# Expert loop of a two-layer encoder: the down product set behind the next block's up product and computed from high and low parts

## What is computed

```python
def expert_block(args):
    xb, e = args
    h = jax.nn.silu(xb @ w_gate[e]) * (xb @ w_up[e])
    return h @ w_down[e]
```

## Time and profile before

| | |
|---|---|
| median of three runs (lowest, highest) | 2327.24 us (2322.62 to 2336.02) |
| the profiled execution's own time | 2328.09 us |
| its span, from first to last instruction | 2326.4 us |
| PE busy, share of the span | 94% |
| DVE, ACT, POOL busy | 57%, 43%, 8% |
| mean granted TensorE clock | 0.967 |
| HBM traffic over the span | 171 GB/s |

### The profile page before, as it was taken

One profiled execution on the slowest core, in us unless ns is written; L12 is line 12 of the kernel. 1 busy time (PEld: TensorE's weight loads), 2 busy tenths in 40 slices (PEclk: granted clock), 3 DMA queues, 4 the chain that ended last, 5 costly groups with the idle time before them and its releaser, 6 DMA issues.

```text
span 2326.4 us, 35484 instructions
## 1 busy us (share of the span) xinstructions
PE 2177.5 (94%) x13296; PEld 1830.2 (79%) x13296; DVE 1320.5 (57%) x2102; ACT 992.8 (43%) x1649; POOL 196.2 (8%) x236
## 2 busy tenths in 40 slices
PE   8899988999999899999788999899999989999998
PEld 7778957989889677777687886598988877777774
DVE  2775476533244766666767746835314466666667
ACT  2355565123332255555235547612323224555553
POOL 0000011000000331000200001100000022200004
PEclk9899989999999899999899999899999989999999
DMA  4045111232100599999511112123211038999996
GB/s 156 37 157 192 37 73 56 73 109 73 56 26 35 193 377 374 380 378 363 209 55 37 37 37 92 38 73 104 78 37 55 37 148 322 376 379 375 379 379 237
DMA packets 78548, 385.64 MB, mean 166 GB/s; under 512 B 10472, under 2 KB 11864, under 8 KB 43608
## 3 DMA queue, kind: packets, MB, share of 16 engines
q1 hardware_dynamic: 55264, 327.83, 37.6%
q0 software_dynamic: 10096, 30.38, 3.6%
q10 hardware_dynamic: 13064, 25.75, 3.0%
HBM read 352.79 MB, written 46.07 MB: 171 GB/s over the span
## 4 chain that ended last, share of the span: by engine, by line
PE 77%; DVE 12%; ACT 7%; issue 2%; DMA 1%; DVEq 0%; POOL 0%; ACTq 0%; SPq 0%; POOLq 0%
PE bank L2116 37%; PE bank L2593 10%; PE bank L2567 9%; PE bank L2557 8%; PE bank L2448 2%; DVE weight_slots_parts L1380 2%; PE bank L2132 2%; PE bank L2402 1%; PE bank L2533 1%; ACT x_transposed L1062 1%; PE bank L2285 1%; ACT weight_slots_parts L914 1%; PE bank L2256 1%; ACT scratch L1018 1%; DVE scratch L1532 1%
## 5 line engine op out<-in xcount | busy, mean ns | idle before, releaser
L2116 PE MATMUL bank<-weight_slots_parts,x_transposed_parts 128*128 128x256 f32 x2496 | 466.6, 289 | 4.5 <-ACT mixer_region L965 2.8
L2116 PEld LDWEIGHTS bank<-weight_slots_parts,x_transposed_parts 128*128 128x128 f32 x2496 | 397.0, 196 | 5.5 <-ACT mixer_region L965 3.2
L1824 DVE TENSOR_TENSOR weight_slots_parts<-weight_slots,mixer_region_parts 128x2048 fp32r<-128x2048 f32 x140 | 321.3, 2314 | 85.9 <-ACT mixer_region_parts L1207 85.8
L1207 ACT ACTIVATE mixer_region_parts<-weight_slots 128x2048 fp32r<-128x2048 f32 x140 | 261.0, 1909 | 23.7 <-ACT x_transposed L1282 18.1
L2116 PE MATMUL bank<-x_transposed_parts,weight_slots_parts 128*128 128x512 f32 (+1 forms) x1024 | 266.5, 348 | 1.8 <-DVE mixer_region L1489 1.8
L1380 DVE TENSOR_TENSOR weight_slots_parts<-weight_slots,weight_slots_parts 128x2048 fp32r<-128x2048 f32 x58 | 132.9, 2292 | 223.5 <-ACT weight_slots_parts L914 223.0
L2593 PE MATMUL bank<-weight_slots,x_transposed 128*128 128x512 f32 x560 | 246.4, 593 | 0.0
L2567 PE MATMUL bank<-mixer_region_parts,x_transposed_parts 128*128 128x256 f32 x1120 | 207.3, 283 | 0.4 <-DVE weight_slots_parts L1824 0.4
L2116 PEld LDWEIGHTS bank<-x_transposed_parts,weight_slots_parts 128*128 128x128 f32 x1024 | 183.4, 196 | 24.4 <-DVE mixer_region L1489 3.3
L2557 PE MATMUL bank<-mixer_region_parts,x_transposed_parts 128*128 128x512 f32 x560 | 193.0, 416 | 5.6 <-DVE x_transposed_parts L1829 5.6
L2593 PEld LDWEIGHTS bank<-weight_slots,x_transposed 128*128 128x128 f32 x560 | 103.4, 190 | 117.9 <-issue 101.7
(11 more groups left out here) (311 smaller groups left out, 3565.7 us busy)
## 6 DMA issues: line engine op xcount, KB each, us to landing
weight_slots<-in_w_gate SPq DMA_DIRECT2D x70, 1024.0 KB, 7.3
weight_slots<-in_w_up SPq DMA_DIRECT2D x70, 1024.0 KB, 7.1
weight_slots<-in_w_down SPq DMA_DIRECT2D x70, 1024.0 KB, 7.6
weight_slots<-in_w_in SPq DMA_DIRECT2D x20, 1024.0 KB, 5.0
slots_y<-x_transposed ACTq DMA_DIRECT2D x66, 256.0 KB, 7.2
weight_slots<-in_wkv_mem SPq DMA_DIRECT2D x16, 1024.0 KB, 4.9
slots_y<-in_consts SPq DMA_DIRECT2D x6, 2304.0 KB, 18.1
weight_slots<-in_w_out SPq DMA_DIRECT2D x8, 1024.0 KB, 5.1
```

What stands on the lines that cost most here:

```text
L1207: nc.scalar.activation(hi, raw, ACT.Copy).then_inc(moe.high_ready, 1)
L1824: v.tensor_tensor(lo, raw, hi.bitcast(F32), ALU.subtract).then_inc(moe.low_ready, 1)
L2116: ins = pe.matmul(ps, lhs[i](k), rhs[j](k), start=k == 0 and a == 0, stop=k == ks - 1 and a == 2)
```

## The change

PE's order in a block becomes gate(b), up(b), the transposes of the next block's rows, down of block b-1, the transposes of `hb` of block b. The first block has no down, and the last one runs gate, down(b-1), up, the transposes, down(b). Down is made of three products of high and low parts like the others, so the two down parts and the turned hidden rows are split as well: ACT makes six high parts in a block and DVE six low ones. Up goes over two halves of the contraction with 512 columns each, in one bank, so the gated product is one instruction. ACT copies both halves of the output. Every raw part of down is loaded when down of block b-1 has let go of its place, one block ahead of its use, except in the last block, whose down parts go into gate's places. `SLOT_ORDER` changes which place the first units of layer 1 use; the loads of layer 1's "q0" and the gather of the stored outputs wait for the shifted counts (`y_stored` by 32 more).

```diff
 
 X_STATS = (50, 58, 84)
+
+DOWN_HI = 3584, G_HI + 2 * KD * KVG
 
...
+SLOT_ORDER = ((0, 1, 2), (1, 0, 2))
 LAST_OF = {key: n for n, (name, key) in enumerate(UNITS)}
 
 
...
         def slot_of(name):
-            return (now[0] * len(UNITS) + UNIT[name]) % SLOTS
+            return SLOT_ORDER[now[0]][UNIT[name] % SLOTS]
...
         hb = xt_t[:, 2560:3072]
-        hbT = xt_t[:, 3072:3584].rearrange("p (k t) -> p k t", k=4)
+        hbT_hi = xt_parts[:, 3072:3584].rearrange("p (k t) -> p k t", k=4)
+        hbT_lo = xt_parts[:, 5632:6144].rearrange("p (k t) -> p k t", k=4)
         yb = xt_t[:, 3584:4608]
...
             o = 4096 * slot_of(("wx0", "wx1", "wx2")[i // 2]) + 2048 * (i % 2)
-            k = (4, 4, KD, KD, 4, 4)[i]
-            return by_k(ring[:, o:o + 2048], k), by_k(ring_parts[:, o:o + 2048], k), by_k(mix_parts[:, 2048 * i:2048 * i + 2048], k)
+            if i < 4:
+                hi = mix_parts[:, 2048 * i:2048 * i + 2048]
+            else:
+                hi = (y_parts, mix_parts)[i - 4][:, DOWN_HI[i - 4]:DOWN_HI[i - 4] + 2048]
+            return by_k(ring[:, o:o + 2048], 4), by_k(ring_parts[:, o:o + 2048], 4), by_k(hi, 4)
...
                     def load_up(e, h, signal):
-                        sp.dma_start(expert_part(2 + h)[0], by_k(w_up[l, e, h])).then_inc(signal, 16)
-
-                    def load_down(e, h, signal):
-                        sp.dma_start(expert_part(4 + h)[0], by_k(w_down[l, e, h], 4)).then_inc(signal, 16)
+                        sp.dma_start(expert_part(2 + h)[0], by_k(w_up[l, e][:, 2048 * h:2048 * h + 2048], 4)).then_inc(signal, 16)
+
+                    def load_down(e, h, signal, part=4):
+                        sp.dma_start(expert_part(part + h)[0], by_k(w_down[l, e, h], 4)).then_inc(signal, 16)
...
                     sp.wait_ge(ids_ready, 1 * l + 1)
                     n_blocks = sp.value_load(r_nbi[0:1, 0:1], min_val=NE, max_val=BLOCKS)
-                    with sp.Fori(1, n_blocks) as b:
+                    sp.sem_inc(moe.dl_loaded, 16)
...
+                    with sp.Fori(1, n_blocks - 1) as b:
+                        e = sp.value_load(r_bei[0:1, bass.ds(b + 1, 1)], min_val=0, max_val=NE - 1)
+                        sp.wait_ge(moe.ga_done, b + 1)
+                        load_gate(e, 0, moe.ga_loaded)
+                        sp.wait_ge(moe.g_filled, b + 2)
+                        load_gate(e, 1, moe.gb_loaded)
+                        sp.wait_ge(moe.ua_done, b + 1)
+                        load_up(e, 0, moe.ul_loaded)
+                        sp.wait_ge(moe.u_filled, b + 2)
+                        load_up(e, 1, moe.ur_loaded)
                         e = sp.value_load(r_bei[0:1, bass.ds(b, 1)], min_val=0, max_val=NE - 1)
-                        sp.wait_ge(moe.ga_done, b)
...
+                        sp.wait_ge(moe.y_filled, 2 * b + 2)
                         load_down(e, 0, moe.dl_loaded)
-                        sp.wait_ge(moe.y_filled, 2 * b + 1)
+                        sp.wait_ge(moe.y_filled, 2 * b + 3)
                         load_down(e, 1, moe.dr_loaded)
+                    e = sp.value_load(r_bei[0:1, bass.ds(n_blocks - 1, 1)], min_val=0, max_val=NE - 1)
+                    sp.wait_ge(moe.ga_done, n_blocks)
+                    load_down(e, 0, moe.ga_loaded, 0)
+                    sp.wait_ge(moe.g_filled, n_blocks + 1)
+                    load_down(e, 1, moe.gb_loaded, 0)
...
+                    def silu(b):
                         act.wait_ge(moe.h_done, b + 1)
                         act.wait_ge(moe.g_filled, b + 2)
                         nc.scalar.activation(gact, banks[2][:, :], ACT.Silu).then_inc(moe.g_ready, 1)
+                    def high_hidden(blocks):
+                        act.wait_ge(moe.hT_filled, blocks + 1)
+                        nc.scalar.activation(hbT_hi[:, :, :], banks[4][:, :].rearrange("p (k t) -> p k t", k=4),
+                                             ACT.Copy).then_inc(moe.hT_high_ready, 1)
+
+                    def store_output(blocks, y_at, h):
+                        if h == 0:
+                            act.wait_ge(moe.y_stored, 32 * blocks + 32)
+                        w = slice(512 * h, 512 * h + 512)
+                        ready = (moe.yl_ready, moe.yr_ready)[h]
+                        act.wait_ge(moe.y_filled, 2 * blocks + 2 + h)
+                        nc.scalar.activation(y_at[:, w], banks[5 + h][:, :], ACT.Copy).then_inc(ready, 1)
+                        act.wait_ge(ready, blocks + 2)
+                        act.dma_start(by_block[blocks - 1, :, w], y_at[:, w]).then_inc(moe.y_stored, 16)
+
+                    def high_down(blocks, part=4):
+                        split_part(part, moe.dl_loaded, blocks + 1)
+                        split_part(part + 1, moe.dr_loaded, blocks + 1)
+
+                    def expert_block(b, first):
+                        if not first:
+                            high_hidden(b)
+                            high_down(b)
+                        silu(b)
+                        split_part(0, moe.ga_loaded, b + 2)
+                        split_part(1, moe.gb_loaded, b + 2)
+                        act.wait_ge(moe.xT_filled, 2 * b + 4)
+                        block_xT()
+                        split_part(2, moe.ul_loaded, b + 2)
+                        if not first:
+                            store_output(b, yb, 0)
+                        split_part(3, moe.ur_loaded, b + 2)
+                        if not first:
+                            store_output(b, yb, 1)
+
+                    expert_block(0, True)
+                    with act.Fori(1, n_blocks - 1) as b:
                         expert_block(b, False)
-                    expert_block(n_blocks - 1, True)
+                    b = n_blocks - 1
+                    high_hidden(b)
+                    high_down(b)
+                    silu(b)
+                    split_part(0, moe.ga_loaded, n_blocks + 1)
+                    store_output(b, yb, 0)
+                    store_output(b, yb, 1)
+                    split_part(1, moe.gb_loaded, n_blocks + 1)
+                    act.wait_ge(spread_turned, l + 1)
+                    act.wait_ge(moe.u_filled, n_blocks + 1)
+                    nc.scalar.activation(spread_t[:, :], banks[0][:, 0:NSPREAD * P], ACT.Copy).then_inc(spread_ready, 1)
+                    high_hidden(n_blocks)
+                    if l < DEPTH - 1:
+                        now[0] = l + 1
+                        split("q0")
+                        now[0] = l
+                    for h in range(2):
+                        store_output(n_blocks, last_yb, h)
+                    if l < DEPTH - 1:
+                        now[0] = l + 1
+                        split("q1")
+                        now[0] = l
...
-                    def expert_block(b, last):
+                    def low_hidden(blocks):
+                        dve.wait_ge(moe.hT_high_ready, blocks + 1)
+                        v.tensor_tensor(hbT_lo[:, :, :], banks[4][:, :].rearrange("p (k t) -> p k t", k=4),
+                                        hbT_hi[:, :, :].bitcast(F32), ALU.subtract).then_inc(moe.hT_ready, 1)
+
+                    def gated(b):
                         dve.wait_ge(moe.g_ready, b + 2)
-                        dve.wait_ge(moe.ul_filled, b + 1)
-                        v.tensor_tensor(hb[:, 0:256], gact[:, 0:256], banks[3][:, 0:256], ALU.mult).then_inc(moe.hl_done, 1)
                         dve.wait_ge(moe.u_filled, b + 2)
-                        v.tensor_tensor(hb[:, 256:512], gact[:, 256:512], banks[7][:, 0:256], ALU.mult).then_inc(moe.h_done, 1)
-                        if not last:
-                            low_block_xT(b + 1)
-                            low_part(0, 4 * b + 5)
...
+                    def expert_block(b, first):
+                        if not first:
+                            low_hidden(b)
+                            low_part(4, 6 * b + 11)
+                            low_part(5, 6 * b + 12)
+                        low_part(0, 6 * b + 13)
+                        gated(b)
+                        low_part(1, 6 * b + 14)
+                        low_block_xT(b + 1)
+                        low_part(2, 6 * b + 15)
+                        low_part(3, 6 * b + 16)
+
...
+                    expert_block(0, True)
+                    with dve.Fori(1, n_blocks - 1) as b:
                         expert_block(b, False)
-                    expert_block(n_blocks - 1, True)
+                    b = n_blocks - 1
+                    low_hidden(b)
+                    low_part(4, 6 * b + 11)
+                    low_part(5, 6 * b + 12)
+                    low_part(0, 6 * b + 13)
+                    low_part(1, 6 * b + 14)
+                    gated(b)
+                    low_hidden(n_blocks)
...
+                    add_stored(0)
+                    add_stored(1)
+                    if l < DEPTH - 1:
+                        low_weights("q0")
```

(103 more changed lines are left out.)

126 lines of the change are left out of this document (37 added, 89 removed).

## The result

The changed kernel takes 2353.61 us (median of 6 runs, 2346.24 to 2357.47) beside 2330.77 for the one before: ratio 1.0093, 95% interval 1.0073 to 1.0113, so 22 us slower. The forecast was 2314, 13 us under the 2327.24 it was made against. The profiled execution took 2348.95 us with a span of 2347.1, against 2328.1 and 2326.4 before: 20.7 us of span to explain.

The account below looks back on a forecast made before the run. PE was taken to bound the expert loop, with DMA near; a period of 18.4 instead of 19.42 us over 31 blocks gave -31.6, first blocks -2, tails +20: 2314.5 from 2328.1, median 2314, range 2290 to 2343.

Parts of the forecast that it names:

- PE's own period, 17.78: In the expert loop, PE's work per block: three products at 5.49 us plus transposes 1.31, 1.64 less than before.
- The chain through one weight part, 11.5 + L: Expert loop, gate's second half released, loaded, split, reused: 11.5 us plus load landing L, taken as 6.8, gives 18.3.
- The DMA bound, 18.2: Expert loop transfers: 7.30 MB a block takes 16.9 us at 431 GB/s; leaving half of today's loss gives 18.2.
- rival C: Expert loop: DMA becomes the bound, period stays 19.3 to 19.4 us, tails unpaid, 2344 us in all; chance 0.2.
- Rival B: Expert loop: the weight part's chain with today's landing, L 7.3 or a bit more, period 18.9, 2330 us; chance 0.2.
- First blocks, -2: First block of each layer: down moves away but the next gate waits for the new chain; -1 us per layer.
- Tails, +20: Ends of both layers: later down, stores and gathers cost +9.2 us in layer 0, 10.5 in layer 1; +12 to +26.
- POOL's scaling at 0: POOL's scaling slows DVE in twelve blocks, at most 12 us; taken as 0 because late low parts have slack.

Follow-up runs that it names:

- experiment 1: Changed kernel with the rows' high part (ACT) and low part (DVE) moved ahead of those of gate's second half: 2306.21 us, ratio 0.9888 to the kernel before.
- experiment 3: Changed kernel with all expert blocks using the rows gathered for the second block, one gather of rows per layer: 2325.75 us, ratio 0.9983 to the kernel before.
- Experiment 7: Against experiment 1, each layer's last block runs gate, up, down of the block before, turn, own down: 2306.20 us, ratio 0.9898 to the kernel before.
- experiment 4: Changed kernel in its pipelined order, but down as before in one fp32 product without high and low parts: 2353.69 us, ratio 1.0078 to the kernel before.
- experiment 6: Against experiment 1, no pipelining: each block's down, in three products, follows its own up and the two turns: 2392.93 us, ratio 1.0270 to the kernel before.
- experiment 2: Changed kernel with one more, unused DVE operation per block ahead of the low part of gate's first half: 2368.72 us, ratio 1.0151 to the kernel before.

## Why the prediction was wrong

- **PE's own period, 17.78: right.** It is 17.7 wherever PE does not wait (experiment 1).
- **The chain through one weight part, 11.5 + L: the mechanism right, its length wrong.** The prediction's sum of the fixed part was 11.5 and the trace has 11.55. It was built on gate's second half; the trace follows the first half, which comes out the same because DVE does both low parts ahead of the rows' one. The step that failed is "so I take 6.8: 18.3", one landing, picked between two medians (7.3 and 4.9), for a load that took 4.9 to 8.8 us. The 29 distances average 19.42, 1.1 over that 18.3. L itself was 7.26 on average, what today's median said: 0.5 of it. In six blocks the distance was longer than the chain, so that short landings did not make up for long ones in full: 0.2. (The 7.7 is the mean of the pieces that were waited for, and so leaves the short ones out.)
- **The clock behind a wait: left out.** It is 0.4 of the 1.1: the load starts 3.59 us behind the gate on average where it is 3.18 at a clock of 1.00.
- **The DMA bound, 18.2: wrong, in the other direction.** 17.7 at 412 GB/s is sustained. The 431 GB/s that the prediction calls sustained is of 3 us; no loop here held it. That the stated size of rival C came true (period 19.3 to 19.4, 2344) is no support for it: its mechanism, the transfers, is refuted by experiment 1. Part of C's place was right: without the gathers of rows gate's load lands 0.6 us sooner and 26 us go (experiment 3). Rival B had the right mechanism and the right mean L; its 18.9 lacks the clock and the six longer blocks.
- **First blocks, -2**: 20.7 and 19.7 (823.69 - 802.96, 1949.22 - 1929.51). The 21.3 and 19.7 that the prediction sets against them are read from the chain, whose gates start up to 0.6 us later than in PE's timeline; there it was 825.88 - 805.11 = 20.8 and 1943.19 - 1924.04 = 19.2. So +0.5 instead of -2: no gain, within its bounds.
- **Tails, +20: 23.6.** Layer 0's +9.2 came out as forecast, with the first gather at 20.1 (forecast 20.9). Layer 1's was 14.5 instead of 10.5. The prediction had PE's later down decide there (8.5 and a bit); the chain of waits runs through the first gathers, which stand 11.9 us further behind the last gate than before, and DVE's additions and normalisations behind them. The slow down, 1.6 us, is part of that. Experiment 7 bears it out: an earlier last down moved the end little in either layer.
- **POOL's scaling at 0**: not tried by itself; experiment 1 has blocks of 17.7 with the scaling in them, so it costs little there.

By terms, in PE's timeline: the 31 distances behind the first ones took 602.4 us, 1.8 less than before in place of 31.6 less, +29.8; first blocks +2.5; ends +3.6; the rest of the program -1.6. That is 34.3 of the 34.5 us between 2314.5 and the profiled 2348.95. The range ended at 2343 since the slow case, C, stood at 2344 with the ends at +20, and was cut there.

## What to carry to other kernels

When the order of a queue is rewritten, follow one buffer all the way round (released, loaded, split, used) and add every instruction that stands ahead of the one that the next stage waits for: here moving the rows' short operations ahead of gate's second half, 2.3 us of DVE's time on the chain, turned 0.9% slower into 1.1% faster. Take a load's landing in such a chain from the same load's rows, with its spread and not as one number: a late landing counts in full, an early one only down to what else holds the block. And let it move: in a full queue the landings grew when the chain got shorter (median 7.2 to 7.9) and shrank when it got longer (6.9). A saving on the engine that bounds (three products for one) and the order that hides its waits have to be judged together with the chain, since each alone measured as a loss: the order with one product of down 0.8% slower (experiment 4), three products without it 2.7% (experiment 6).

## What was not expected of the hardware

- The mean DMA share was 0.97 to 1.01 at 366, 381 and 412 GB/s alike. Worked out from the weights' queue, 8 KB took 335 to 338 ns in the changed kernel, 345 to 347 in experiment 3 and 317 to 319 in experiment 1: packets filled the time that was there.
- After waits of 1.8 to 2.9 us PE often ran at a granted clock near its lower level while busy (0.59 over 4 us), and 48 matmuls took 12.8 instead of 11.2 us; others, of 1.89, 1.95 and 2.34 us, and of 2.82 us in experiment 2, had no such effect (1.00). After 3.75 us (experiment 1's last block) one down took 8.25 us, at 0.50, instead of 5.5 to 5.8:

```profile
1080.05 8.25 PE bank L2608 x24
```
